# A two-branch decoder step: the compression stage rebuilt, with its weights and rows requested earlier and new rows stored over six rounds

## The reference, cut to what matters

```
h = rmsnorm(x) * (1 + scale) + shift ; u = h @ w_in       # 48 column sets of 128, besides keys/values
def compress(kv, pe, w1, w2):                              # for k and for v
    blocks = kv.reshape(b, l // 64, 64, g, d) + pe
    flat = blocks.transpose(0, 1, 3, 2, 4).reshape(b, l // 64, g, 64 * d)
    return silu(flat @ w1) @ w2                            # 4096 -> 128 -> 64
lg = q @ k + bias[t5_bucket(distance)]                     # three softmaxes: compressed, selected, window
o = g0 * o_cmp + g1 * o_sel + g2 * o_win
x += gate * (concat(o * silu(z_a), conv(h) * silu(z_c)) @ w_out) ; final rmsnorm
```

## Time and profile before

| | us |
|---|---|
| Time, median of three runs (1655.50, 1658.26, 1662.54) | 1658.26 |
| The profiled execution's own time | 1658.38 |
| Its span in the profile | 1656.5 |
| TensorE busy (92% of the span) | 1527.3 |
| VectorE busy | 720.8 |
| ScalarE busy | 605.5 |
| Start to the first matmul of the third column set | 0 to 165.3 |
| Projection rounds, to the last matmul | to 708.9 |
| Compression and keys, to the main loop's first matmul | 708.9 to 865.1 |

### The profile page before, as it was taken

How to read it: one execution, slowest core, us unless ns; L and a number is a source line. 1 busy time by engine, 2 the same in 40 slices (tenths; PEclk the granted TensorE clock), 3 DMA queues, 4 the chain that set the end, 5 groups by cost and what they waited for, 6 DMA issues and landing times.

```text
span 1656.5 us, 25563 instructions
## 1 busy us (share of the span) xinstructions
PE 1527.3 (92%) x10098; PEld 1321.3 (80%) x10098; DVE 720.8 (44%) x1773; ACT 605.5 (37%) x1231; POOL 201.3 (12%) x380
## 2 busy tenths in 40 slices
PE   5997999999999999959959999999999988799996
PEld 1887999999999999958847777777777766588884
DVE  2540221313123131245557677667676654543221
ACT  2430111110111111124456676666666645521110
POOL 1104000000000000021011122122121131000000
PEclk9999999999999999979979999999999999799998
DMA  9707432332222323187120121111011049662320
GB/s 345 127 27 270 114 103 78 78 90 65 77 78 69 99 53 89 40 267 242 57 85 26 33 75 30 31 44 39 27 47 32 20 152 292 205 193 91 100 67 20
DMA packets 164936, 164.62 MB, mean 99 GB/s; under 512 B 48685, under 2 KB 146029, under 8 KB 159505
## 3 DMA queue, kind: packets, MB, share of 16 engines
q1 hardware_dynamic: 150800, 96.66, 21.9%
q0 software_dynamic: 14016, 66.32, 11.8%
HBM read 131.27 MB, written 35.83 MB: 101 GB/s over the span
## 4 chain that ended last, share of the span: by engine, by line
PE 84%; DVE 6%; DMA 5%; ACT 2%; issue 2%; SPq 1%; POOL 0%; DVEq 0%; ACTq 0%; POOLq 0%
PE PS L975 33%; PE PS L1314 11%; PE PS L1130 8%; PE PS L1098 7%; PE PS L1076 4%; PE PS L1023 4%; PE PS L1077 3%; DMA wr<-in_w_in 2%; PE PS L937 1%; PE PS L938 1%; PE PS L939 1%; PE PS L1170 1%; DMA wor<-in_w_out 1%; DMA adaw<-in_ada_w 1%; PE PS L1015 1%
## 5 line engine op out<-in xcount | busy, mean ns | idle before, releaser
L975 PE MATMUL PS<-hhi,wh 128*128 128x352 f32 x1152 | 251.2, 326 | 9.1 <-issue 8.5
L975 PE MATMUL PS<-hhi,wl 128*128 128x352 f32 x1152 | 248.7, 323 | 0.0
L975 PE MATMUL PS<-hlo,wh 128*128 128x352 f32 x1152 | 248.4, 324 | 0.0
L1479 ACT ACTIVATE pr<-PS,nm 128x640 f32<-128x640 f32 (+7 forms) x256 | 179.8, 704 | 81.9 <-DVE nm L1815 78.1
L975 PEld LDWEIGHTS PS<-hhi,wh 128*128 128x128 f32 x1152 | 196.0, 189 | 13.0 <-issue 11.6
L975 PEld LDWEIGHTS PS<-hhi,wl 128*128 128x128 f32 x1152 | 198.2, 188 | 0.0
L975 PEld LDWEIGHTS PS<-hlo,wh 128*128 128x128 f32 x1152 | 196.0, 188 | 0.0
L1499 ACT ACTIVATE ptt<-PS 128x512 f32<-128x512 f32 x222 | 128.0, 596 | 73.0 <-PE PS L1098 72.8
L1098 PE MATMUL PS<-ident,pr 128*128 128x128 f32 x1056 | 147.3, 274 | 0.0
L1692 DVE TENSOR_TENSOR wl<-wr,wh 128x1024 fp32r<-128x1024 f32 x48 | 58.6, 1220 | 187.5 <-ACT wh L1395 187.0
L1130 PE MATMUL PS<-ptt,kvt 128*64 128x256 f32 x1056 | 136.1, 389 | 1.1 <-DVE ptt L1855 0.7
(11 more groups left out here) (317 smaller groups left out, 2314.2 us busy)
## 6 DMA issues: line engine op xcount, KB each, us to landing
wr<-in_w_in SPq DMA_DIRECT2D x32, 512.0 KB, 7.6
adaw<-in_ada_w SPq DMA_DIRECT2D x8, 1024.0 KB, 9.7
wr<-in_w_in SPq DMA_DIRECT2D x32, 256.0 KB, 3.7
qb<-q_stacked SPq DMA_DIRECT2D x32, 256.0 KB, 3.1
mr<-mixed SPq DMA_DIRECT2D x16, 512.0 KB, 3.9
mixed<-ych POOLq DMA_DIRECT2D x8, 528.0 KB, 3.3
z_attn_silu<-zab POOLq DMA_DIRECT2D x8, 528.0 KB, 2.9
xb<-in_x_prompt POOLq DMA_DIRECT2D x8, 512.0 KB, 7.8
```

The lines of the kernel that those rows point to most:

```text
L975: ins = pe.matmul(PS[:, bank + c, 0:CH], a[kind % 2][:, k, :], b[:, k, c * CH:(c + 1) * CH], start=(k == 0 and b is hhi and a is wh), stop ...
L1479: act.activation(pr[r][:, h, 0:k], score_cols(b0, w), ACT.Exp, scale=-1.0, bias=nm[:, r, h:h + 1], accum_out=rsum[:, r, h:h + 1]).then_inc ...
```

## The change

Parts, all in one program:

- **Opening.** SP requests column set 2 directly behind sets 0 and 1, and set 3 behind two pieces of `gw`, where before all four pieces (and the end of the keys/values products) stood ahead of set 2. POOL stores only `p_kc` and `p_vc` ahead of round 0; the others go one per round, in rounds 0 to 3 (`store_rows(2 + j)`), 3 (`store_sample`), 4 and 5 (`store_window`).
- **Compression's data.** The key weights `w1[0]` are loaded in round 3, the prompt's key rows (`xp4[0]`, one array for all 64 positions, cleared by VectorE in round 2) in rounds 4 to 7. The value rows `xp4[1]` (cleared by POOL), `w2`, two constants and `w1[1]` are requested together when the rounds end.
- **Loop.** The prompt's rows are turned in two transposes for eight turns, in place of eight. `xt` has two buffers of four steps. VectorE copies the prompt's columns of four steps in one strided instruction, and each step's copies are 256 columns instead of 273. Steps 4 and on of the keys write where `qhi` and `qlo` and the stored tails lie, so both copying engines wait at step 4 for `q_st` and `out_st`.
- **Attention's keys** are turned and split inside the loops, in 16 pieces of 64 x 512, `key_high` and `key_low`, with turns at steps 1, 9, 17 of the keys and 5 of the values. The last of value compression comes after the first four scores.
- The sigmoid of the branch gates moves to round 1. The bias table is stored negated (`rows` times -1), so `near` isn't negated and the sample's additions become subtractions.

```diff
             load_w(0, 0, True)
             load_w(0, 1, True)
+            load_w(0, 2, False)
             sp.wait_ge(kv_mm, 2 * NTT)
...
-            for k in range(4):
+            for k in range(2):
+                sp.dma_start(gw[k][:, :], ada3[:, k, 2 * D:3 * D]).then_inc(adaw_ld[k], 16)
+            load_w(0, 3, False)
+            for k in (2, 3):
...
             sp.wait_ge(p2_mm, 8 * NK)
+            sp.wait_ge(w_lo, 8 * NK)
+            sp.wait_ge(xz, 2)
+            for r in range(4):
+                load_rows(1, r)
...
+            for q in range(4):
+                load_w1(1, q)
             sp.wait_ge(x3_t, 80)
...
-            sp.wait_ge(c3_mm, 2)
+            sp.wait_ge(x3_t, 128)
...
+            def load_rows(c, r):
+                rows_, pe_ = ((p_kc, cmp_pe_k), (p_vc, cmp_pe_v))[c]
+                for g in range(NG):
+                    for e in range(2):
+                        sp.dma_start(xp4[c][32 * r:32 * r + NPB, :, g, 64 * e:64 * e + 64],
+                                     flat(rows_, (2 * r + e) * DKV + HD * g, [(BLK * DKV, NPB), (8 * DKV, 8), (1, HD)])).then_inc(xp_ld[c], 16)
...
+            def turn(c, t):
+                q, n = t // 16, 64 * c + t
+                if t % 16 == 0:
+                    pe.wait_ge(xq_ld[q], 32 * (c + 1))
+                if t == 0:
+                    pe.wait_ge(xp_ld[c], 384)
+                if n == 3:
+                    pe.wait_ge(p2_ev[1], 24)
+                if n >= 4:
+                    pe.wait_ge(xe[t % 2], n // 2 - 1)
...
+                if t % 8 == 0:
                     for g in range(NG):
+                        pe.transpose(PS[:, 0, 2 * P + P * g:3 * P + P * g], xp4[c][:, t // 8, g, :], ident[:, :])
...
+            def turn_keys(f):
+                if f >= 2:
+                    pe.wait_ge(kt_lo, 4 * (f - 1))
...
+                    if n == 4:
+                        dve.wait_ge(q_st, 16 * 32)
+                        dve.wait_ge(out_st, nout[0])
+                    if n >= 8:
+                        dve.wait_ge(x3_mm, n - 7)
+                    if m % 4 == 0:
...
+                        dve.tensor_copy(xt[m // 4 % 2][:, :, :, 2 * P:CB].rearrange("p r g b -> p g r b"),
+                                        PS[:, 0, 2 * P:4 * P].rearrange("p (g r b) -> p g r b", g=NG, b=32)[:, :, :, 0:NPB + 1])
...
+                    if c == 0 and m % 2 and m >= 11:
+                        if m < 31:
+                            key_low((m - 11) // 8, (m - 11) // 2 % 4)
+                        else:
+                            key_low(2, 2)
+                            key_low(2, 3)
```

More of the change, by code:

```diff
@@ L731, in _ @@
                 nout[0] += 16 * 9
+            store_rows(0)
+            store_rows(1)
             def gather_quarter(c, q):
@@ L762, in _ @@
             gather_quarter(0, 1)
+            po.memset(xp4[1][:, :, :, :], 0.0).then_inc(xz, 1)
             po.wait_ge(out_st, nout[0])
@@ new lines, in _ @@
+            turn(0, 0)
+            turn(0, 1)
+            pe.wait_ge(xp_ld[2], 64)
+            for m in range(32):
+                if m in (1, 9, 17):
+                    turn_keys(m // 8)
+                if m < 31:
+                    turn(0, 2 * m + 2)
+                    turn(0, 2 * m + 3)
+                pair(0, m)
+            turn(1, 0)
+            turn(1, 1)
+            pe.wait_ge(w2_ld, 64)
+            pe.wait_ge(kt_lo, 12)
+            pe.wait_ge(hs_rdy, 1)
+            for g in range(NG):
+                pe.matmul(PS[64 * g:64 * g + 64, 6, 0:2 * P], w2[0][:, 0:64], hs3[:, g, 0:2 * P], start=True, stop=True)
@@ L1061, in scores @@
+            for g in range(NG):
+                ins = pe.matmul(PS[:, 7, NPB * g:NPB * g + NPB], w2[0][:, :], hs3[:, g, 2 * P:2 * P + NPB], start=True, stop=True)
+            ins.then_inc(c3_mm, 1)
+            pe.wait_ge(xp_ld[3], 64)
+            for m in range(32):
+                if m == 5:
+                    turn_keys(3)
+                if m < 31:
+                    turn(1, 2 * m + 2)
+                    turn(1, 2 * m + 3)
+                pair(1, m)
             def scores(w, h):
@@ L1743, in _ @@
                     ev(j, kind)
+                    if j == 2 and kind == 3:
+                        dve.wait_ge(g_st, 16)
+                        dve.memset(xp4[0][:, :, :, :], 0.0).then_inc(xz, 1)
                 if j == 1:
@@ L1761, in _ @@
                     ins.then_inc(xe[0], 1)
+                    if c == 0 and m % 2 and m >= 11:
+                        if m < 31:
+                            key_low((m - 11) // 8, (m - 11) // 2 % 4)
+                        else:
+                            key_low(2, 2)
+                            key_low(2, 3)
+                    if c == 1 and m % 2 and 15 <= m < 23:
+                        key_low(3, (m - 15) // 2)
+                    if c == 1 and m == 24:
+                        link(dve.memset(qbd[:, :, :], 0.0))
+                        for g in range(NG):
+                            half = slice(64 * g, 64 * g + 64)
+                            ins = dve.tensor_copy(qbd[half, :, 32 * g:32 * g + 32].rearrange("p b (j t) -> p b j t", t=TS),
+                                                  qs[half, :, :].rearrange("p j (b t) -> p b j t", t=TS))
+                        ins.then_inc(q5_rdy, 1)
@@ L1875, in _ @@
                 if w == 0:
-                    keys_low(1)
                     factors(0)
-                    dve.wait_ge(nr_rdy, 4)
+                    dve.wait_ge(c3_mm, 2)
+                    dve.wait_ge(c3_hi, 2)
+                    for q in range(2):
+                        dve.tensor_copy(vcs[:, 4 * q:4 * q + 4, :], PS[0:NSB, 6 + q, :].rearrange("p (b c) -> p b c", c=DKV)).then_inc(c3_ev, 1)
             for w in range(NI):
```

287 lines of the change are left out of this document (129 added, 158 removed).

## The result

| | before | changed |
|---|---|---|
| Median of the first runs, us | 1656.90 (4 runs) | 1609.12 (4 runs) |
| Ratio, 95% interval | | 0.9702, 0.9683 to 0.9722 |
| Median when measured again, us | 1658.84 | 1603.24 |
| Ratio, 95% interval | | 0.9662, 0.9643 to 0.9682 |
| Span of the profiled executions, us | 1656.5 | 1606.0 and 1604.2 |

The two measurements, on two occasions, bracket the forecast of 1604. Their intervals just fail to overlap (0.9683 against 0.9682), so the same kernel differed by 0.4% between them: what follows treats differences under 0.4% between measurements taken apart as nothing.

The account below looks back on a forecast made before the run. TensorE, busy for 92% of the span, was taken to bound the kernel, leaving holes, cold stretches and dropped matmuls to gain. Terms -10.1 - 12.9 - 4.2 - 1.0 - 4.2 - 21.9 = -54.3 took 1658.4 to 1604 us, range 1598 to 1616.

Parts of the forecast that it names:

- opening: Kernel start: third column set requested earlier, so TensorE's hole of 8.5 us and cold 1.6 go: -10.1 us.
- entry: From the last round to the key loop: first product begins at 712.7 and not 725.61, -12.9 us.
- key loop: Steps of 1.364 us with four transposes, plus waits and cold clock: 49.8 against 54.0 us, -4.2.
- value loop: Same shorter steps plus one key turn and `qbd` work: 45.6 against 49.8 us, -4.2.
- end: Last value product to main loop's first matmul: 7.4 us against 29.3, -21.9, with key pieces moved into the loops.
- Step 4: Key loop: this step's copies wait until the tails are stored, costing 0.7 us (0 to 1.7).
- the gather: Key loop, turn 16: wait for the second quarter of past rows requested by POOL, 1.4 us (0 to 4).
- step 17: Key loop: the key turn waits for four `key_low` pieces from VectorE, 0.7 us (0 to 1).
- The cold clock at the entry: Key loop start: clock may be low after 2.6 us of holes, costing 1.0 us (0 to 2.5).
- Value weights late: Rival before the value loop: SP's rows and `w1[1]` held up by gathers, +3 to +11 us, 1607 to 1615; chance 0.15.
- Runs of 256 bytes: Value row loads: trace read as 2.2 us per set against 2.64 in 512-byte runs, disagreeing with the skill's doubled cost.
- VectorE's room: Loops: four steps have 0.6 us of room; row copy of x us adds (x - 0.9) x 16; slower-kernel rival's chance 0.02.

Follow-up runs that it names:

- the kernel with the order undone: Changed kernel with the opening's request order as before (third set behind four gate pieces), stores still spread over the rounds: 1606.22 us, ratio .9683.
- the kernel with weights, then rows: Changed kernel with tails stored earlier and SP requesting w2 and constants, then value weights, then value rows: 1610.82 us, ratio .9712.
- the run with five copies: Changed kernel with VectorE making the strided row copy four times more at each of its 16 places: 1612.61 us, ratio .9729.

## Why the prediction was right

By its own terms, in us, from the two profiles of the changed kernel against the one of the kernel before:

| term | predicted | first | second |
|---|---|---|---|
| start, up to the rounds' first product | 0 | -0.8 | +0.5 |
| opening | -10.1 | -9.9 | -9.9 |
| entry, 16.74 before | -12.9 | -13.2 | -13.1 |
| key loop, 54.0 before | -4.2 | -1.8 | +1.6 |
| keys to values, 6.3 | -1.0 | -1.6 | -1.9 |
| value loop, 49.8 | -4.2 | -2.5 | -4.1 |
| end, 29.3 | -21.9 | -22.7 | -22.6 |
| main loop and what follows | 0 | +2.1 | -2.8 |
| sum | -54.3 | -50.5 | -52.3 |

The three large terms, 44.9 of the 54.3, came within 0.8 us each, by the mechanism that was named: a set requested early, rows that are there when the rounds end, pieces that lie beside TensorE's loop. A step took 1.36 as predicted. The experiments show the mechanisms of the opening and of most of the end; the entry rests on the trace alone. That the second median lies within 1 us of the forecast is partly luck: by the spans the stage was forecast 2.4 and 4.1 us too short, and the rest moved by +2.1 and -2.8 on its own. (The lowest sum, with every wait at its low bound, is 1604.1 - 3.8 = 1600.3 and not 1600.5, which changes nothing.)

**Key loop.** The mis-sized term. Its work was put at 46.0 and its waits and cold clock at 3.8; first profile 47.0 and 5.1, second 55.6 in all. Step 4 (0.7 predicted), the gather (1.4) and step 17 (0.7) waited 1.04, 2.35 and 0.53 in the first and 0, 1.19 and 0.53 in the second. Missing from the sum were the lag at step 8 and the 4.12 for constants that stand behind the value rows in SP's queue, with some 2 us of slow clock behind it (0.58 from 753.5 to 757.5). The wait for the constants was no single event: the kernel with the order undone has it too, 3.88. The cold clock at the entry, put at 1.0, came in the second profile and cost 1.6 (3.51 us from the first product to the second, 1.90 in the first profile); in the first it didn't come. The sum added it to step 4's wait, but each profile has only one of the two.

**Value weights late.** The first profile has this rival, at its place and smaller than its +3 to +11: a wait of 1.77, of which all but 0.26 lies beside the copies that the first value product waits for anyway (4.72 against 4.46), and 1.6 of cold clock behind it (0.50 to 0.90 of full speed from 758 to 764). In the old clock the prediction had the weights landed at 760, which is about 750 here; they landed at 748.27 + 9.75 = 758.02. The term that was too small is SP's time for the value rows. It was priced by bytes, and SP took 29.2 us to issue their 24 requests.

**Runs of 256 bytes.** This step was wrong. I took the window 408 to 414 for the ZA set in 256-byte runs and 444 to 448 for a set in runs of 512 bytes. The queue's packets in these two windows of the kernel before say the reverse (queue: packets, MB, share of 16 engines):

```profile
q1 hardware_dynamic: 1040, 0.52, 31.1%
```

```profile
DMA packets 2080, 0.52 MB, mean 131 GB/s; under 512 B 2080, under 2 KB 2080, under 8 KB 2080
...
q1 hardware_dynamic: 2080, 0.52, 65.6%
```

The first has 1040 packets and 1.87 us of the 16 engines' time for 0.52 MB, the second 2080 packets, all under 512 B, and 2.62 us: 1.4 times as much for the same bytes. In the full stretch, 722 to 738, the changed kernel (value rows) and then the kernel with weights, then rows (weights in that stretch):

```profile
q1 hardware_dynamic: 1465, 0.34, 17.4%
```

```profile
q1 hardware_dynamic: 1578, 0.79, 17.2%
```

About as many packets take the same time, 2.8 us, and carry 0.34 MB in the one and 0.79 in the other: in this stretch a small packet costs what one of twice its size does. The late weights deserved a higher chance than I left them. The Trainium skill (DMA: Bandwidth & Descriptors, Specifications) asks for 512 bytes at least for the full rate. The trace agrees with it, where the prediction said that it disagrees.

**VectorE's room** was wrong too, 0.16 us in one step instead of 0.6 over four. It changed nothing, as the row copy took 0.21 to 0.30. By this room (an estimate from the run with five copies) a slower copy would have shown from 0.37 us on and not from 0.9, and the kernel would have come out even at 0.37 + 54.3 / 16, about 3.8 us, not 4.3.

**Main loop.** The 2.1 us by which it was longer in the first profile is no effect of the change: over twelve profiles with the same instructions the rest took 787.6 to 793.5.

## What to carry to other kernels

Two measures against the same wait are not added: here, with the traffic gone the order of requests was worth nothing, and with the order right the hole was gone with the traffic still there. Where a stretch has its DMA queues full, as here, moving a request moved the wait to whatever was then last, so count the bytes and the requests of the stretch before ordering them, and request small constants ahead of it. Before crediting an edit with a wait that is gone, look whether a second profile of the unchanged kernel has that wait. An engine's slack counts within the step whose result is waited for, not as a mean over the steps around it.

## What the runs showed of the hardware that was not expected

- A request's issue on SP can block for long while gathers run: 27.29 us for four requests of 512 KB. A constant of half a kilobyte, requested at 742.4, landed 9.7 us later.
- Back-to-back copies of 128 x 136 on VectorE start every 0.21 us though each is shown as 0.30.
- In two of twelve profiles, both with the queues full, VectorE or ScalarE started step 8 late and held TensorE for 1.20 and 3.14 us, although by the records the turns were made and nothing in the program was left to wait for. It wasn't there when the changed kernel was profiled again. Its cause stays open.
- Eleven of the twelve profiles have the same holes on TensorE at the entry, 1.79 and 0.53 us. The granted clock from 704 to 708 was 1.00 in four of them and 0.61 to 0.86 in seven.
